# One fused transformer kernel on one Trainium2 core: relative-bias products issued singly among the first block's projection products, in place of runs between them

## What is computed

```
mod = silu(c) @ w_ada + b_ada                    # six parts of 1024
h   = rmsnorm(x) * (1 + sc_m) + sh_m             # and hc for the context
(na_k, na_v, ml_k, ml_v, ml_g, na_q, ...) = split(h @ w_in)
bias  = rpb[:, dr, dc]                           # relative bias, 8 heads
s_loc = where(mask, q . k + bias, -1e30)         # neighbourhood scores
```

## Time and profile before

| what | value |
| --- | --- |
| timed runs | 2398.29, 2391.03, 2397.14 us; median 2397.14 |
| profiled execution, own time | 2394.06 us |
| its span in the profile | 2391.8 us |
| TensorE (PE) busy | 2209.9 us, 92% |
| VectorE (DVE) busy | 928.2 us, 39% |
| ScalarE (ACT) busy | 713.0 us, 30% |
| granted TensorE clock, mean | 0.972 of 2.4 GHz |
| memory traffic | 626.99 MB, 262 GB/s on average |

### The profile page before, as it was taken

How to read it: one execution, slowest core, us unless ns; L and a number is a source line. 1 busy time by engine, 2 the same in 40 slices (tenths; PEclk the granted TensorE clock), 3 DMA queues, 4 the chain that set the end, 5 groups by cost and what they waited for, 6 DMA issues and landing times.

```text
span 2391.8 us, 33084 instructions
## 1 busy us (share of the span) xinstructions
PE 2209.9 (92%) x13876; PEld 1574.2 (66%) x13876; DVE 928.2 (39%) x1357; ACT 713.0 (30%) x953; POOL 35.5 (1%) x60
## 2 busy tenths in 40 slices
PE   6999988998898889888988899999999799999998
PEld 4888786333333333333333498998999689998997
DVE  4655575221111111111111365465444464574453
ACT  4123443211111111111111345444433444544432
POOL 2100010000000000000000000000000000000000
PEclk8899999999999999999999999999999899999999
DMA  9663335899999999999999744543543454543542
GB/s 350 232 210 106 103 97 174 362 427 428 426 428 427 427 427 428 427 427 424 428 428 428 295 147 149 170 148 138 177 167 133 152 167 141 168 151 141 176 160 88
DMA packets 136597, 626.99 MB, mean 262 GB/s; under 512 B 7775, under 2 KB 30831, under 8 KB 111615
## 3 DMA queue, kind: packets, MB, share of 16 engines
q1 hardware_dynamic: 128688, 605.67, 64.9%
q0 software_dynamic: 7168, 18.97, 2.7%
q10 hardware_dynamic: 591, 0.13, 0.0%
HBM read 623.69 MB, written 1.05 MB: 261 GB/s over the span
## 4 chain that ended last, share of the span: by engine, by line
PE 68%; DMA 23%; DVE 3%; issue 3%; ACT 2%; SPq 0%; ACTq 0%; DVEq 0%
DMA ring<-in_w_lin 20%; PE bank L1586 15%; PE bank L1675 12%; PE bank L1910 11%; PE bank L1925 5%; PE bank L1833 3%; PE bank L1306 3%; PE bank L1256 2%; DMA ring<-in_w_in 2%; PE bank L1699 1%; PE bank L1852 1%; PE bank L1684 1%; PE bank L1241 1%; PE bank L1453 1%; PE bank L1360 1%
## 5 line engine op out<-in xcount | busy, mean ns | idle before, releaser
L1586 PE MATMUL bank<-ring,arenaA 128*64 128x512 f32 x3072 | 692.7, 601 | 39.0 <-DMA ring<-in_w_lin 28.4
L1586 PEld LDWEIGHTS bank<-ring,arenaA 128*64 128x64 f32 x3072 | 211.1, 138 | 461.5 <-issue 390.5
L2463 DVE TENSOR_TENSOR ring_rounded<-ring,ring_rounded 128x2048 fp32r<-128x2048 f32 (+1 forms) x160 | 338.1, 2153 | 145.0 <-ACT ring_rounded L951 145.0
L951 ACT ACTIVATE ring_rounded<-ring 128x2048 fp32r<-128x2048 f32 (+1 forms) x160 | 280.3, 1799 | 277.1 <-DMA ring<-in_w_in 109.0
L1675 PE MATMUL bank<-arena_rounded,ring_rounded 128*128 128x256 f32 x2496 | 309.3, 284 | 0.0
L1675 PEld LDWEIGHTS bank<-arena_rounded,ring_rounded 128*128 128x128 f32 x2496 | 301.5, 190 | 4.1 <-issue 3.1
L1910 PE MATMUL bank<-arena_rounded,ring_rounded 128*128 128x256 f32 x2112 | 257.4, 283 | 0.9 <-DVE arena_rounded L2653 0.5
L1910 PEld LDWEIGHTS bank<-arena_rounded,ring_rounded 128*128 128x128 f32 x2112 | 254.0, 191 | 4.7 <-ACT arena_rounded L1093 4.0
L2409 DVE TENSOR_SCALAR arenaA<-bank 128x512 f32<-128x512 f32 x32 | 22.1, 692 | 502.8 <-PE bank L1586 502.8
L932 ACT ACTIVATE arenaA<-bank 128x512 f32<-128x512 f32 x32 | 19.1, 597 | 328.4 <-PE bank L1631 328.4
L1925 PE MATMUL bank<-arena_rounded,ring_rounded 128*128 128x256 f32 x912 | 109.9, 283 | 2.3 <-DVE arenaA L2665 2.3
(11 more groups left out here) (399 smaller groups left out, 2208.1 us busy)
## 6 DMA issues: line engine op xcount, KB each, us to landing
ring<-in_w_down SPq DMA_DIRECT2D x64, 2048.0 KB, 21.9
ring<-in_w_gate SPq DMA_DIRECT2D x64, 2048.0 KB, 23.0
ring<-in_w_lin SPq DMA_DIRECT2D x64, 2048.0 KB, 25.5
ring<-in_w_in SPq DMA_DIRECT2D x35, 2048.0 KB, 11.6
ring<-in_w_ffn_gate SPq DMA_DIRECT2D x10, 2048.0 KB, 8.1
ring<-in_w_ffn_up SPq DMA_DIRECT2D x10, 2048.0 KB, 7.7
ring<-in_w_ffn_down SPq DMA_DIRECT2D x12, 1536.0 KB, 6.4
arenaA<-in_w_ada POOLq DMA_DIRECT2D x16, 1024.0 KB, 5.9
```

Source lines behind the costliest of these rows:

```text
L951: act.activation(place2(name + "_hi", ringR)[:, a:b, :], place2(name)[:, a:b, :], ACT.Copy).then_inc(w_hi, 1)
L1586: last = pe.matmul(bank[b][k * SLOTS:(k + 1) * SLOTS, :], lhsT(c), slot(j)[:, c % 4, k * 512:(k + 1) * 512], start=False, stop=(c == DC - ...
L2463: dve.tensor_tensor(place2(name, ringR)[:, a:b, :], w[:, a:b, :], hi[:, a:b, :], ALU.subtract).then_inc(w_lo, 1)
```

## The change

The function that issued a run is replaced by `rel_one(b, j)`, which issues product j of run b, with the same waits ahead of a run's first product and the same count behind its last. `tokens` and `features` call it inside their loops, behind every second projection product, until ten are out: behind c = 1, 3, 5, 7 of the first part (j = 0 to 3), of the second (4 to 7), and c = 1, 3 of the third (8, 9). The seven groups are the ones behind which the runs stood; `ml_v0` has four products, all in its first part. Nothing else differs.

```diff
-            def rel_group(b):
-
-                if b == 0:
+            def rel_one(b, j):
+
+                k = 10 * b + j
+                if k >= min(10 * b + 10, 64):
+                    return
+                if k == 0:
                     pe.wait_ge(relrhs_set, 1)
-                if b >= 2:
+                if j == 0 and b >= 2:
                     pe.wait_ge(rel_copied, b - 1)
-                for k in range(10 * b, min(10 * b + 10, 64)):
-                    if k in (0, 32):
-                        slab(f"rel{k // 32}")
...
-                last.then_inc(rel_done, 1)
+                if k in (0, 32):
+                    slab(f"rel{k // 32}")
...
+                last = pe.matmul(bank[4 + b % 2][:, 48 * j:48 * j + 48], sl[0:63, k % 32, :], relrhs[0:63, :], start=True, stop=True)
+                if k == min(10 * b + 10, 64) - 1:
+                    last.then_inc(rel_done, 1)
...
                     for c in range(DC):
                         last = pe.matmul(b[:, :], h(c), w[:, c, :], start=(part == 0 and c == 0), stop=(part == 2 and c == DC - 1),
                                          skip_group_check=True)
+                        if f"{nm}{t}" in REL_IN and c % 2 and part * DC + c < 20:
+                            rel_one(REL_IN[f"{nm}{t}"], part * 4 + c // 2)
                 last.then_inc(lin_done, 1)
-                if f"{nm}{t}" in REL_AFTER:
-                    rel_group(REL_AFTER[f"{nm}{t}"])
```

More of the change, by code:

```diff
@@ L1206, in ada_fold @@
                 last.then_inc(lin_done, 1)
-            def rel_group(b):
-                if b == 0:
+            def rel_one(b, j):
[3 more added lines that the diff above has]
+                if k == 0:
                     pe.wait_ge(relrhs_set, 1)
-                if b >= 2:
+                if j == 0 and b >= 2:
                     pe.wait_ge(rel_copied, b - 1)
-                for k in range(10 * b, min(10 * b + 10, 64)):
-                    if k in (0, 32):
-                        slab(f"rel{k // 32}")
-                    sl = ring[:, (S1[f"rel{k // 32}"] % RING) * SLAB:][:, 0:4096].rearrange("p (k q) -> p k q", k=32)
-                    last = pe.matmul(bank[4 + b % 2][:, 48 * (k - 10 * b):48 * (k - 10 * b) + 48], sl[0:63, k % 32, :],
-                                     relrhs[0:63, :], start=True, stop=True)
-                last.then_inc(rel_done, 1)
-            REL_AFTER = {"na_v0": 0, "na_v1": 1, "na_v2": 2, "na_v3": 3, "ml_k0": 4, "ml_k1": 5, "ml_v0": 6}
+                if k in (0, 32):
+                    slab(f"rel{k // 32}")
+                sl = ring[:, (S1[f"rel{k // 32}"] % RING) * SLAB:][:, 0:4096].rearrange("p (k q) -> p k q", k=32)
+                last = pe.matmul(bank[4 + b % 2][:, 48 * j:48 * j + 48], sl[0:63, k % 32, :], relrhs[0:63, :], start=True, stop=True)
+                if k == min(10 * b + 10, 64) - 1:
+                    last.then_inc(rel_done, 1)
+            REL_IN = {"na_v0": 0, "na_v1": 1, "na_v2": 2, "na_v3": 3, "ml_k0": 4, "ml_k1": 5, "ml_v0": 6}
             bothHi = lambda c: hBoth[:, :, c, :]
@@ L1271, in features @@
                                          stop=(part == 2 and c == DC - 1), skip_group_check=True)
+                        if name in REL_IN and c % 2 and part * DC + c < 20:
+                            rel_one(REL_IN[name], part * 4 + c // 2)
                 last.then_inc(lin_done, 1)
-                if name in REL_AFTER:
-                    rel_group(REL_AFTER[name])
             for t in range(2):
```

## The result

The changed kernel takes 2402.67 us (median of seven runs, 2401.2 to 2408.83), the kernel before, in the same session and the earlier one, 2395.86 (seven runs, 2391.03 to 2399.94). The ratio is 1.0039 with a 95% interval of 1.0029 to 1.0050: slower by about 9.3 us (6.9 to 12.0), where 8.7 had been forecast. The two medians themselves are 6.8 us apart, the two profiled executions 8.6. The profiled execution of the changed kernel took 2402.67 us, with a span of 2400.4.

The account below looks back on a forecast made before the run. TensorE was taken to bound the stretch: edges +18.1 us, clock giving back up to 9.4, waits 0, net +8.7 on bases of 2394.06 and 2397.14, middle 2404.3 us; range 2397 to 2413.

Parts of the forecast that it names:

- The price of a product: Single relative-bias product between projection products: pays both edges, 0.54 us against 0.255 in a run; bounds 0.22 and 1.08.
- The stretch: From na_v0's first projection product to ml_v1's second: 77.4 us at full clock, against 68.7 before.
- The clock: TensorE in the stretch: no fall to half clock, giving back up to 9.4 us lost in six groups.
- rivals D and E: D: clock falls behind some L1205 runs, +10 to +15, chance 0.15; E: 1.2 GHz throughout, +48 or more, chance 0.03.
- Waits: Semaphore waits, bank copies and queues around the stretch: move along with the products, 0 us, bounds -0.8 and +0.8.
- The end: Behind the stretch to the kernel's end: nothing is set from outside, so the whole 8.7 us passes on.
- Rival B: Weight loads taken ahead when a product stands alone: 0.22 us each, stretch 57.1, -11.6 us, 2384; chance 0.08.
- Rival C: Way out of a product cheaper in mid-group: 0.43 us a product, +1.6 us, 2397; chance 0.10.

Follow-up runs that it names:

- single96: The changed kernel with relative-bias products, still issued singly, reading 96 rows in place of 63: 2378.35 us, beside 2398.16 for the kernel before.
- single128: The changed kernel with relative-bias products, still issued singly, reading 128 rows in place of 63: ratio to the kernel before 0.9958.
- twos: The changed kernel with 63-row products issued two at a time behind every fourth projection product: 2389.92 us, beside 2392.05 for the kernel before.
- fives: The changed kernel with 63-row products issued five at a time, behind a group's 8th and 16th projection products: ratio to the kernel before 0.9980.

## Why the prediction was right

- **The price of a product.** Forecast 0.54 us, put together from the edges of a run. Measured (77.88 - 39.2 - 3.6)/64 = 0.55. The crossings 0.32 each and 0.22 a product, which the same rows give, held from 64 crossings down to 13.
- **The stretch.** Forecast 77.4 us, measured 77.9; the difference of 9.2 against 8.7 is the 0.01 us more a product. The time forecast was 2404.3, the median is 2402.67.
- **The clock.** No fall was forecast and none came, also not behind the L1205 runs, so rivals D and E are out for this execution; the other six timed ones have 0.975 to 0.977 as mean clock of the whole, beside 0.977 of this one. That the clock would give back 9.4 us was right in sum, since the kernel before had the same 20 us of low time when it ran again. Where the argument reads as if each full run brings one fall of 1.6 us, it was wrong: the second execution of the kernel before has a full run without one. Six equal groups in one profile looked like a rule and weren't.
- **Waits.** VectorE's copies, the roundings and the transfers moved along without a new wait of TensorE, and the 0.8 us at L1205 stayed.
- **The end.** +9.2 in the stretch, +10.0 at the first expert, +8.6 in the span, 9.3 by the ratio and 6.8 by the medians: to within the spread it passed through whole.
- **Rival B** (loads ahead when a product stands alone) is out for 63 rows, and is what happens with 96 or 128. The Trainium skill's TensorE: Matmul & The Clock Gate, "Part 2: What happens when you issue a matmul", has the next weights load under the running product. The runs agree with it for 96 and 128 rows (load 0.23 us ahead) and not for 63 (together with its product). The same page of the Trainium skill, "Part 3: Packing small matmuls — row/col tiling", has loads overlap only when the row group differs; by the traces of single96 and single128, loads overlap where the rows are shared.
- **Rival C** (the way out is cheap without the waits of a group's start) is out: within groups it is 0.20 and 0.33 as at their start.

## What to carry to other kernels

When small products are to be mixed with large ones on TensorE, read the start-to-start times at the edges of a run, not those within it: what a run pays twice, interleaving pays for every product. Look at whether the loader (PEld) is idle ahead of the small product. If it is, and the operands can be read with the rows of their neighbours at no cost, zeros behind the real ones, do so (96 rows were enough here; 64 aren't, by the rows of L1360); here this turned a loss of 9 us into a gain of 12.

Where the rows can't be matched, keep runs of small products short enough that the clock stays, and no shorter: twos and fives both beat single products here. And take falls of the clock from more than one execution, as a total over a stretch: their number and places change.

## What was not expected

- A 96-row product among 128-row ones costs no more than a 128-row one (stretch 57.12 against 57.13 us), while one of 63 rows costs 0.32 us more each time (77.88).
- Reading 128 rows in place of 63 in runs left where they were went with less time at the low clock, 6 and 3 us in two executions against 20 and 20, which was worth more (6 to 8 us of stretch) than the seven crossings (2.2). Why is open.
- Weights of 64 rows, and a change from 64 to 128 columns, have the same late loads in rows that were in the trace before the change.
- The kernel before had a mean clock of 0.87 over the stretch in both executions, with the low time in different groups.
